# Modulation sums of a hybrid decoder trunk, moved from TensorE to VectorE

## The reference

```python
c_act = jax.nn.silu(c)
for l in range(DEPTH):
    mod = (c_act @ ada_w[l] + ada_b[l])[:, None, :]        # 6 x 1024 columns
    sh_m, sc_m, g_m, sh_f, sc_f, g_f = jnp.split(mod, 6, axis=-1)
    hm = rms_norm(x, norm_mix_g[l]) * (1.0 + sc_m) + sh_m
    proj = hm @ w_in[l]                                     # 1024 x 2728
    z, xbc, dt_raw, cq, ckv, krope, mq, mk, mv = jnp.split(proj, split_at, axis=-1)
    y = jnp.concatenate([ssd(z, xbc, dt_raw), mla(cq, ckv, krope), moba(mq, mk, mv)], axis=-1) @ w_out[l]
    x = x + g_m * y
    hf = rms_norm(x, norm_ffn_g[l]) * (1.0 + sc_f) + sh_f
    x = x + g_f * moe_ffn(hf, ...)                          # 16 experts, 2 for each token
```

## Time and profile before

| | us |
|---|---|
| median of 3 executions | 1655.88 |
| lowest, highest | 1654.44, 1656.6 |
| the profiled execution, its own time | 1650.8 |
| its span, first to last instruction | 1648.8 |

### The profile page before, as it was taken

The page is one execution under the profiler, slowest core; times in us unless marked ns, Lnnn a source line. Parts: engine busy times, 40 slices in busy tenths (PEclk is TensorE's granted clock), DMA queues, the critical chain, the costliest instruction groups (busy, mean ns, idle before and its releaser), DMA issues. The chain is left out here.

```text
span 1648.8 us, 16262 instructions
## 1 busy us (share of the span) xinstructions
PE 1470.1 (89%) x6255; PEld 1038.2 (63%) x6255; DVE 844.3 (51%) x1073; ACT 603.5 (37%) x843; POOL 136.9 (8%) x206
## 2 busy tenths in 40 slices
PE   8599989998859999999958998899796899999991
PEld 3388765666646666666526886647574666666660
DVE  0662065544557665566257413655545665566642
ACT  1432222462325444555114313326412544554520
POOL 0100013000100000000010000120000000000002
PEclk9699998998969999999978999899997899999996
DMA  9621443301649999998765217070127699999944
GB/s 334 246 83 60 159 150 119 137 1 51 232 177 354 384 381 379 380 383 324 271 250 218 67 56 258 1 255 1 51 83 288 233 381 381 378 385 383 382 166 179
DMA packets 152409, 371.03 MB, mean 225 GB/s; under 512 B 6265, under 2 KB 8935, under 8 KB 151688
## 3 DMA queue, kind: packets, MB, share of 16 engines
q1 hardware_dynamic: 137000, 313.30, 52.4%
q0 software_dynamic: 15328, 56.63, 8.9%
HBM read 336.09 MB, written 33.82 MB: 224 GB/s over the span
## 5 line engine op out<-in xcount | busy, mean ns | idle before, releaser
L1578 DVE TENSOR_TENSOR ring_rounded<-ring,mod_rounded 128x2048 fp32r<-128x2048 f32 (+1 forms) x54 | 102.5, 1929 | 109.1 <-ACT mod_rounded L1220 109.1
L1578 DVE TENSOR_TENSOR work_rounded<-work,mod_rounded 128x2048 fp32r<-128x2048 f32 (+1 forms) x48 | 91.3, 1929 | 103.9 <-ACT mod_rounded L1220 103.9
L960 PE MATMUL ps<-mod_rounded,work_rounded 128*128 128x512 f32 x340 | 138.6, 408 | 3.9 <-DVE work_rounded L1695 3.9
L962 PE MATMUL ps<-mod_rounded,work_rounded 128*128 128x512 f32 x340 | 135.4, 398 | 0.0
L980 PE MATMUL ps<-ring,work 128*128 128x512 f32 x288 | 126.8, 593 | 1.4 <-ACT work L1243 1.4
L676 PE MATMUL ps<-ring,csil 128*128 128x512 f32 x256 | 117.8, 620 | 0.0
L961 PE MATMUL ps<-ring_rounded,work_rounded 128*128 128x512 f32 x288 | 114.3, 397 | 0.0
L980 PE MATMUL ps<-work 128*128 128x512 f32 x256 | 112.5, 592 | 0.0
L961 PE MATMUL ps<-work_rounded 128*128 128x512 f32 x256 | 101.1, 395 | 0.0
L1086 ACT ACTIVATE work<-ps 128x512 f32<-128x512 f32 (+1 forms) x48 | 26.4, 551 | 186.4 <-PE ps L721 119.1
L721 PE MATMUL ps<-ring_rounded,actT_rounded 128*128 128x512 f32 (+1 forms) x256 | 93.5, 365 | 0.0
(11 more groups left out here) (297 smaller groups left out, 2988.1 us busy)
## 6 DMA issues: line engine op xcount, KB each, us to landing
ring<-in_ada_w SPq DMA_DIRECT2D x22, 2048.0 KB, 8.3
ring<-in_moe_w_gate SPq DMA_DIRECT2D x18, 2048.0 KB, 9.8
ring<-in_moe_w_up SPq DMA_DIRECT2D x18, 2048.0 KB, 11.2
ring<-in_moe_w_down SPq DMA_DIRECT2D x18, 2048.0 KB, 10.4
work<-in_moe_w_gate SPq DMA_DIRECT2D x16, 2048.0 KB, 9.8
work<-in_moe_w_up SPq DMA_DIRECT2D x16, 2048.0 KB, 11.4
work<-in_moe_w_down SPq DMA_DIRECT2D x16, 2048.0 KB, 10.4
ring<-in_w_in SPq DMA_DIRECT2D x10, 2048.0 KB, 9.3
```

The source lines that it names most:

```text
L960: pe.matmul(ps[j][:, :], xl, hi, start=k == 0, stop=False)
L962: mm = pe.matmul(ps[j][:, :], xh, hi, start=False, stop=k == KD - 1)
L1578: v.tensor_tensor(slots_r[3 * odd + j][:, 512 * k0:512 * k1], slots[3 * odd + j][:, 512 * k0:512 * k1], buf.bitcast(F32), ALU.subtract).th ...
```

## The change

The sums of twelve blocks (4 to 11 of this layer, 0 to 3 of the next) are formed on DVE during the input product. In the last layer the sums of the "next" layer are formed too, and not used. DVE scales the weight rows of a partition by `csil` and adds the eight row groups into an accumulator (two of 512 columns, in the tile `gain`), and adds the bias on one partition. PE then sums over the partitions with one matmul by `ones`, ACT copies one row out of PSUM, POOL stores four rows at a time in DRAM (`mod_rows`), and SP loads them from there, broadcast to all partitions, where the bias was loaded before. The sums' weights use slot 0 in two halves of 1 MB; W_in, and later W_out, have slots 1 and 2. In the diff `load_ada` is SP's, `ada_total` PE's, `ada_row_out` ACT's and `ada_sum` DVE's; the load of a W_in block two places on in the order waits for PE's last group of the block that its slot held. The exponential of softplus and the latent squares move up to behind group 15, the logarithm behind group 18.

```diff
-    mixer_loads = [("in", b) for b in IN_ORDER] \
-        + [("ada", 4), ("ada", 5), ("mla", 0)] + [("ada", b) for b in range(6, 11)] \
-        + [("out", 0), ("out", 1), ("ada", 11)]
+    RING = {("in", b): 1 + i % 2 for i, b in enumerate(IN_ORDER)}
+    RING.update({("mla", 0): 0, ("out", 0): 1, ("out", 1): 2})
+    NADA = 12
+    ADA_AFTER = {5: 0, 7: 1, 10: 2, 11: 3, 13: 4, 14: 5, 17: 6, 18: 7, 21: 8}
+    ADA_ADDS = KD + 1
+    def ada_added(m, half):
+        return ada_sm, ADA_ADDS * m + (KD // 2) * (half + 1)
...
+                def load_ada(m):
+                    layer, b = ada_block(m, L)
+                    for half in range(2):
+                        if m:
+                            sp.wait_ge(*ada_added(m - 1, half))
+                        src = A["ada_w"][bass.ds(layer, 1), 512 * half:512 * half + 512, 512 * b:512 * b + 512]
+                        sp.dma_start(ada_half[half], src.rearrange("l (k p) n -> p (l k) n", p=P)).then_inc(ada_ld[half], 16)
...
+                load_ada(0)
+                load("in", IN_ORDER[2])
+                load_ada(1)
+                load_ada(2)
+                load("in", IN_ORDER[3])
+                for m in (3, 4, 5):
+                    load_ada(m)
+                load("in", IN_ORDER[4])
+                for m in (6, 7, 8):
+                    load_ada(m)
+                load("in", IN_ORDER[5])
+                for m in (9, 10, 11):
+                    load_ada(m)
...
+                def ada_total(m):
+                    pe.wait_ge(*ada_total_ready(m))
+                    if m >= 2:
+                        pe.wait_ge(ada_row, m - 1)
+                    pe.matmul(ps[6 + m % 2][:, :], ones, ada_acc[m % 2], start=True, stop=True).then_inc(ada_ps, 1)
...
-                ada(4)
-                ada(5)
+                        if n in ADA_AFTER:
+                            ada_total(ADA_AFTER[n])
...
+                def ada_row_out(m):
+                    a.wait_ge(ada_ps, m + 1)
+                    p0 = 32 * (m % 4)
+                    a.activation(ada_bias_row(m), ps[6 + m % 2][p0:p0 + 1, :], ACT.Copy).then_inc(ada_row, 1)
...
+                def ada_sum(m):
+                    acc, p0 = ada_acc[m % 2], 32 * (m % 4)
+                    if m >= 2:
+                        v.wait_ge(ada_ps, m - 1)
+                    for k in range(KD):
+                        if k % 4 == 0:
+                            v.wait_ge(ada_ld[k // 4], 16 * (m + 1))
+                        w = ada_half[k // 4][:, k % 4, :]
+                        if k:
+                            add(v.scalar_tensor_tensor(acc, w, csil[:, k:k + 1], acc, ALU.mult, ALU.add))
+                        else:
+                            add(v.tensor_scalar(acc, w, csil[:, 0:1], None, ALU.mult))
...
+                    v.tensor_tensor(acc[p0:p0 + 1, :], acc[p0:p0 + 1, :], ada_bias_row(m), ALU.add).then_inc(ada_sm, 1)
...
+                conv(0)
+                conv(1)
+                ada_sum(0)
+                conv(2)
+                conv(3)
+                conv(4)
+                ada_sum(1)
+                in_weights_lo(2)
+                conv(5)
+                conv(6)
+                conv(7)
+                ada_sum(2)
+                ada_sum(3)
+                in_weights_lo(3)
+                ada_sum(4)
+                ada_sum(5)
                 in_weights_lo(4)
```

More of the change, by code:

```diff
@@ L184, in trunk, with ada_bias_row @@
     hfrow = view(12288, T, D)
+    ada_half = [ring[:, 0, 2048 * j:2048 * j + 2048].rearrange("p (k n) -> p k n", k=4) for j in range(2)]
+    ada_acc = [gain[:, 512 * j:512 * j + 512] for j in range(2)]
+    yt_sq = view(s0 + 6144, 512)
+    def ada_bias_row(m):
+        return biasm[32 * (m % 4):32 * (m % 4) + 1, m // 4, :]
     def h_row(base, t):
@@ L277, in trunk @@
     next_ev = sem("next_ada_block_out")
+    ada_ld = [sem(f"ada_half{j}_loaded") for j in range(2)]
+    ada_b_ld = sem("ada_bias_rows_loaded")
+    ada_sm = sem("ada_products_added")
+    ada_ps = sem("ada_row_in_psum")
+    ada_row = sem("ada_row_out")
+    row_st = [sem(f"ada_rows_stored{j}") for j in range(3)]
     modb_ld = sem("mod_bias_loaded")
@@ L532, in trunk @@
     y_col = [0, 128, 256, 384, CQ0, CQ0 + 128, MQ0, MQ0 + 128]
-    base_ld = [16 * (last_load[j] // 3 + 2) + (16 if (load_no[("mla", 0)] + 1) % 3 == j else 0) for j in range(3)]
+    base_ld = [32 + 16, 64 + 16, 64 + 16]
     def expert_loaded(e, odd, j):
@@ L546, in _, with load @@
             def _(sp):
[L547 to L555, removed]
+                def load(what, b):
+                    slot, loaded = slots[RING[what, b]], slot_ld[RING[what, b]]
+                    if what == "in":
+                        i, w = IN_ORDER.index(b), in_width[b]
+                        if i >= 2:
+                            sp.wait_ge(*read_by_pe("in", IN_ORDER[i - 2]))
                         src = A["w_in"][bass.ds(L, 1), :, 512 * b:512 * b + w].rearrange("l (k p) n -> p (l k) n", p=P)
@@ L583, in _ @@
                     sp.dma_start(hpar[:, n, :], A[name][bass.ds(L, 1)].broadcast_to([P, NH])).then_inc(par, 16)
[L584 to L599, removed]
+                load("in", IN_ORDER[1])
@@ new lines, in _ @@
+                for j in range(3):
+                    load_ada_bias(j)
+                load_ada(0)
[11 more added lines that the diff above has]
+                    load_ada(m)
@@ new lines, in _ @@
+                load("mla", 0)
+                load("out", 0)
+                load("out", 1)
+                sp.wait_ge(acc_ps, w_in_read)
+                sp.wait_ge(row_st[0], 16)
+                sp.wait_ge(row_st[1], 16)
+                sp.dma_start(mod[:, 2 * D:], mod_rows[bass.ds(L, 1), 2 * D:].broadcast_to([P, 4 * D])).then_inc(modb_ld, 16)
+                sp.wait_ge(ada_ps, NADA)
+                sp.dma_start(gain[:], A["norm_ffn_g"][bass.ds(L, 1)].broadcast_to([P, D])).then_inc(gain_ld, 16)
@@ L610, in load_expert @@
                                  ).then_inc(slot_ld[n], 16)
-                for j in range(2):
-                    sp.wait_ge(*slot_read(last_load[j]))
-                    load_expert(j, j, 0)
+                sp.wait_ge(qkv_ps, 2 * T)
+                load_expert(0, 0, 0)
+                sp.wait_ge(*read_by_pe("out", 0))
+                load_expert(1, 1, 0)
                 sp.wait_ge(wo_ev, 8)
@@ L618, in _ @@
                     load_expert(3 + j, j, 1)
[L619 removed]
+                sp.wait_ge(*read_by_pe("out", 1))
                 load_expert(2, 2, 0)
@@ L859, in _ @@
                 pe.wait_ge(h_dn, 3)
-                for b in range(6, 10):
-                    ada(b)
                 pe.wait_ge(qkv_ev, 2 * T)
-                pe.wait_ge(ada_ev, 6)
                 turn_qk(0)
@@ L1341, in _, with conv @@
                 v.wait_ge(pads, 2)
-                for f in range(8):
+                def conv(f):
                     v.wait_ge(win_ev, f + 1)
```

178 lines of the change are left out of this document (87 added, 91 removed).

## The result

| | before | after |
|---|---|---|
| median of 5 executions, us | 1654.44 | 1671.21 |
| lowest, highest | 1649.73, 1656.6 | 1665.32, 1678.21 |
| profiled execution: its span | 1648.8 | 1676.5 |

The ratio is 1.0106, with a 95% interval of 1.0073 to 1.014: the change makes the kernel slower by 17 us.

The account below looks back on a forecast made before the run. TensorE was busy 89%, but VectorE's free 80 us in the input product, equal to the new sums, left no slack. 2 x 21.2 cost - 26.1 gain = +16.3, with clock +19.3: 1675 us median, range 1649 to 1697.

Parts of the forecast that it names:

- The stage of the sums: Input product: VectorE's sums and load waits start the chunk scan 20.1 us later, costing 21.2 us a layer.
- A half landed in 5.2 us: Sums' weights: a 1 MB reload, interpolated between two traced loads at 5.2 us, loses 1.5 us at five sums.
- Third, and dearest, those loads stand in SP's queue behind the halves: Input product: W_in blocks 4 and 5 issue only after sums 4 and 7; TensorE stops 12 us, VectorE waits 4 and 6.
- the prediction breaks if the halves don't hold back SP's queue: Sign against the forecast, in the input product: three of its waits were said to hang on that queue.
- Rival C: Input product: reload waits vanish, W_in waits of 4 and 6 us stay; stage costs 11 us, total near 1651; chance 0.12.
- That VectorE had no slack: Input product: twelve sums of 6.6 us make 80 us, exactly VectorE's free time there.
- Rival B: Input product: VectorE keeps up, loads arrive in time; stage costs 1 us a layer, total 1632; chance 0.08.
- Blocks 6 to 9: Behind the chunk scan, ahead of attention: VectorE's last squares start earlier, gaining 8.4 us a layer, not 27.6.
- Block 10: It covers POOL's rstd; without it the normalisation starts earlier, gaining 3.4 us a layer.
- Block 11: Routing: gains nothing, since TensorE behind it still waits 2.3 us for VectorE's expert choice.
- End of layer 0: Sums hidden by the combine; only VectorE's four additions after it go, gaining 2.5 us once.
- Clock: TensorE idle before work, after blocks 6 to 10 fall away, lowers the granted clock: 1.5 us a layer lost.

Follow-up runs that it names:

- two_queues: The changed kernel with the halves' loads issued by POOL on its own queue and W_in's by SP alone; 1664.88 us, ratio 1.0065.
- the gap alone: The kernel before, without the products, loads and additions of blocks 6, 7 and 8; 1637.33 us, ratio 0.9885.
- eight_sums: The changed kernel with eight sums on VectorE instead of twelve, the next layer's blocks 0 to 3 back on TensorE at layer end; 1645.61 us, ratio 0.9955.
- six_warm: The changed kernel with six sums, blocks 6 and 7 on TensorE before attention, three initial W_in slots, constant matmuls behind attention and in routing; 1614.94 us, ratio 0.9764.
- w_in_ahead: The changed kernel with only SP's load order altered, each W_in load ahead of the halves it stood behind; 1676.98 us, ratio 1.015.
- warm: The changed kernel with matmuls of constants in TensorE's idle stretches ahead of and behind the attention and in the routing; 1667.67 us, ratio 1.0083.
- no_reload: The changed kernel with the sums' weight halves loaded once a layer and all twelve sums made from them; 1792.23 us, ratio 1.0847, with other experts chosen.
- eight_ahead: The changed kernel with eight sums on VectorE and each W_in load ahead of the halves; 1642.56 us, ratio 0.9942.
- eight_two_queues: The changed kernel with eight sums on VectorE and the halves' loads on POOL's own queue; 1630.57 us, ratio 0.9844.
- eight_two_warm: The kernel of eight_two_queues with matmuls of constants ahead of and behind the attention and in the routing; 1627.59 us, ratio 0.9828.

## Why the prediction held, and where it did not

The total held: +19.3 was forecast for a like execution, +16.8 is what the medians show. The stage that decides came out as worked out; in the rest several terms were off and cancelled, and that is luck.

- **The stage of the sums**, 21.2 us a layer, 20.1 of them up to the scan, measured +22.2 and +19.5 up to the scan. The steps came one by one: sum 4 done at 163.8 (forecast 160, and the stage began 2.2 later), index 4's load out then, TensorE's stop 10.9 (12), VectorE's waits 3.5 and 6.5 (4 and 6), the latent copies ending at 242.3 (238.1 and the 2.2 make 240.3). A half landed in 5.2 us, as interpolated. The fit of the Trainium skill (DMA: Bandwidth & Descriptors, Anatomy of one DMA), an estimate of 4.4 us for this size, is stated there for loads that GpSimd issues, and the prediction set it against SP's. The trace agrees for neither: 5.2 from SP, and 5.7 from GpSimd in two_queues.
- **"Third, and dearest, those loads stand in SP's queue behind the halves"** is the step that failed as a cause. The waits stood where I put them, but taking them away bought nothing at layer 0's scan (168.9 and 164.8 against 165.6). Halves and W_in were priced as separate waits. In the runs they are one account: when W_in no longer holds VectorE, the reloads do, which then take 19.2 us instead of 9.5. That the prediction breaks if the halves don't hold back SP's queue, "since three of its waits hang on that", was wrong. Rival C, in which the reload waits vanish and those for W_in stay, had it the wrong way round; its price was off too, since 1655.9 - 4 with the 3 us of clock is 1655 and not 1651.
- **That VectorE had no slack** was the step that decided, and it is shown for its program as it is ordered: four sums less (26 us) brought 13.3 and 11.1 us in the two layers until TensorE was last, and no reloads 19.4 and 17.4.
- **Rival B** priced the stage without these waits as level with before but for a column sum of 1 us. Without reloads it is 146.2 against 143.4.
- **Blocks 6 to 9**: 8.4 forecast, 10.1 and 9.9 measured, 9.8 in the run of the gap alone. I left POOL's chain as it stood, and it became 1.1 us shorter, 11.0 us instead of 12.1. Before, the addition of block 6 held VectorE, so that two of its squares ran beside POOL's products, and the two products that they met took 1.30 and 1.36 us instead of 0.32. After, only one does. The timelines of POOL and VectorE, first before, then after:

```profile
278.66 1.22 DVE L1460 TENSOR_TENSOR work<-work 128x1024 f32<-128x1024 f32 x1
278.76 1.30 POOL L1779 TENSOR_TENSOR work<-actT,cst 128x64 f32<-128x64 f32 x1
...
281.21 1.36 POOL L1777 TENSOR_TENSOR work<-work,cst 128x64 f32<-128x64 f32 x1
```

```profile
298.32 1.36 POOL L1847 TENSOR_TENSOR work<-actT,cst 128x64 f32<-128x64 f32 x1 [9.04 <-ACT work L1178]
299.65 0.31 POOL L1848 TENSOR_TENSOR work<-actT,cst 128x64 f32<-128x64 f32 x1
...
298.28 1.23 DVE L1537 TENSOR_TENSOR work<-work 128x1024 f32<-128x1024 f32 x1 [0.80 <-ACT work L1178]
```

  The Trainium skill (SBUF — State Buffer, SBUF: two separate sides) says that the two engines share a port pair which one takes for a whole instruction, VectorE when it reads two operands from SBUF while GpSimd reads from there too. By that rule POOL's product waits for the multiplication of 1.23 us to end, and the trace agrees: 1.36 beside it, 0.31 without.

- **Block 10**: the mechanism is there. The normalisation follows POOL's rstd at once:

```profile
391.48 1.64 POOL L1803 TENSOR_TENSOR sml<-sml,cst 128x8 f32<-128x8 f32 x1
393.15 1.23 DVE L1622 TENSOR_TENSOR work<-work,sml 128x1024 f32<-128x1024 f32 x1 [5.80 <-POOL sml L1803]
```

  where it was 3.4 us late before. But of the 3.4 only 0.2 arrived, since the attention ahead of it took 3.2 longer (69.7 us to its last squares instead of 66.5), at a clock of 0.86 instead of 0.96.
- **Block 11**: no gain, as forecast; TensorE's wait for VectorE's choice is now 9.4 us.
- **End of layer 0**: 2.5 forecast, 6.7 measured. The four additions went. And the load of the fourth block, 2 MB issued at 822.3, no longer runs beside the gathers of the expert rows, of which the first is issued at 823.0 (the other three blocks had landed by 816.8). From that issue to the first combination it is 6.5 us instead of 9.5. In eight_sums, where the load is back, a gather again lands 7.7 to 8.3 us after its issue, against 4.3 to 6.5 in the changed kernel. I had counted the adds and not what their loads collide with.
- **Clock**: 1.5 us a layer forecast; scan, attention and routing lost 7.6 together in layer 0, one us of it the column sum, at granted clocks of 0.89, 0.86 and 0.65 instead of 0.95, 0.96 and 0.82. That all of the rest is the clock is likely and not shown. Here the term was too small, and it is the one that differs between executions. The row that it came from, 12.6 us at 0.77, holds 5.8 us at 1.2 GHz and not 3; they cost 2.9.

## What to carry to other kernels

Free time of an engine is not capacity when the moved work brings its own stream of loads: price the buffer first, here 5.2 us of reload beside 3.8 us of work. When two streams wait for two engines on one queue, reordering may only exchange their waits; here it took fewer sums, or no reloads, to remove them. And free time counts only where the engine's own order has work for it: VectorE stood still for 8 to 10 us with sums left to do. Move just what fits a measured idle stretch, as two blocks of seven us in a gap of twenty.

## What the runs showed of the hardware

The clock differs for the same program at the same place. In the profile of six_warm, the scan of layer 0 took 40.9 us and that of layer 1 44.0. Their first 8.6 us, as windows:

```profile
210.40:219.00 8.60, 7.25 (x54) 6.83 (x54) 4.84 (x6) 2.75 (x5) 1.65 (x2) 0.92 0.81 283
...
994.40:1003.00 8.60, 8.55 (x46) 8.09 (x46) 3.84 (x5) 1.98 (x4) 1.66 (x2) 0.66 0.86 307
```

The granted clock is 0.92 in the one and 0.66 in the other, and TensorE had stood idle 2.8 and 2.7 us ahead of the last column sum before each, and 0.4 and 1.1 behind it. In w_in_ahead, too, the attention took 76.0 us in layer 0 and 78.1 in layer 1, the routing 34.0 and 35.6. Four to seven such differences of 1.5 to 3 us would be the 11 us by which the two profiled spans lie further apart than the medians; that they are the cause is likely and not shown.

The scan shows more of what a standstill has to do with it. In the changed kernel, w_in_ahead, warm, two_queues and no_reload TensorE stood idle 7.0 to 10.0 us ahead of it; all ten scans began at a clock of 0.67 to 0.78 (the first 8.6 us) and took 42.0 to 44.3 us. In eight_sums, eight_ahead, eight_two_queues and eight_two_warm it stood idle 1.33 us; all eight began at 1.00 and took 40.1 to 41.4. So part of the 2.7 us that the scan lost goes with the wait for VectorE ahead of it. After short stops both occur, as in six_warm, and what sets off the low clock there stays open.
